# Four of 32 counting rounds moved from the opening of the sample attention to the steps behind its last keys

## What is computed

```
score = where(admissible, sum_h wi * relu(qi . ki) * IDX_SCALE, -inf)
_, sel = top_k(score, 256)
s = where(sel_valid, q . k[sel] * HEAD_DIM ** -0.5, -inf)
o = softmax(s) @ v[sel]
```

## Time and profile before

| | |
|---|---|
| median of 3 runs | 2613.73 us (2608.51 to 2617.16) |
| profiled execution | 2612.9 us |
| its span | 2611.0 us |
| sample attention | about 330 to 519 us of the span |
| PE busy in the whole span | 96% |
| DVE, ACT, POOL busy in the whole span | 61%, 40%, 4% |

### The profile page before, as it was taken

One profiled execution on the slowest core, in us unless ns is written; L12 is line 12 of the kernel. 1 busy time (PEld: TensorE's weight loads), 2 busy tenths in 40 slices (PEclk: granted clock), 3 DMA queues, 4 the chain that ended last, 5 costly groups with the idle time before them and its releaser, 6 DMA issues. The chain is left out here.

```text
span 2611.0 us, 47343 instructions
## 1 busy us (share of the span) xinstructions
PE 2518.6 (96%) x18617; PEld 2407.9 (92%) x18648; DVE 1604.3 (61%) x2965; ACT 1055.0 (40%) x1732; POOL 106.9 (4%) x135
## 2 busy tenths in 40 slices
PE   8899988899999999999999999989999999999998
PEld 7799956577899999999999999989999999999998
DVE  6667876777557666666534466764766666663422
ACT  5567686586534322222312343553422232231201
POOL 1310023200000000000000000000000000000000
PEclk9899999999999999999999999999999999999999
DMA  6312389820123222222513213234142222261312
GB/s 206 86 49 76 113 303 372 331 95 1 34 84 105 74 81 77 85 76 74 207 56 102 86 57 111 72 90 160 59 134 77 74 74 74 74 223 38 113 49 77
DMA packets 256893, 282.59 MB, mean 108 GB/s; under 512 B 18856, under 2 KB 212650, under 8 KB 248557
## 3 DMA queue, kind: packets, MB, share of 16 engines
q1 hardware_dynamic: 244893, 205.09, 24.5%
q0 software_dynamic: 11776, 75.50, 7.9%
q10 hardware_dynamic: 80, 0.02, 0.0%
HBM read 226.51 MB, written 54.06 MB: 107 GB/s over the span
## 5 line engine op out<-in xcount | busy, mean ns | idle before, releaser
L1138 PE MATMUL ffn_acc<-trunk_x_ahead,trunk_w_hi 128*128 128x272 f32 x2464 | 470.6, 290 | 1.0 <-PEq L87 1.0
L1138 PE MATMUL ffn_acc<-ffn_x_later,ffn_w_hi_more 128*128 128x272 f32 x2112 | 398.0, 287 | 5.4 <-DVE ffn_t_u L950 3.4
L1138 PEld LDWEIGHTS ffn_acc<-trunk_x_ahead,trunk_w_hi 128*128 128x128 f32 x2464 | 389.2, 190 | 1.1 <-issue 1.1
L1138 PE MATMUL ffn_acc<-trunk_x_ahead,trunk_w_lo 128*128 128x272 f32 x1232 | 356.0, 289 | 0.0
L1188 PE MATMUL ffn_acc<-trunk_x_ahead,trunk_w_hi 128*128 128x364 f32 (+1 forms) x1344 | 346.4, 327 | 0.7 <-DVE ffn_x_later L1073 0.7
L1138 PEld LDWEIGHTS ffn_acc<-ffn_x_later,ffn_w_hi_more 128*128 128x128 f32 x2112 | 331.9, 189 | 6.3 <-issue 6.2
L1138 PE MATMUL ffn_acc<-ffn_x_later,ffn_w_lo_more 128*128 128x272 f32 x1056 | 304.4, 288 | 0.0
L1188 PE MATMUL ffn_acc<-trunk_x_ahead,trunk_w_lo 128*128 128x364 f32 (+1 forms) x768 | 251.0, 327 | 0.0
L1085 DVE TENSOR_TENSOR trunk_xT<-ffn_acc,trunk_xT 128x364 f32<-128x364 f32 x144 | 76.3, 534 | 274.4 <-PE ffn_acc L1188 274.4
L1188 PEld LDWEIGHTS ffn_acc<-trunk_x_ahead,trunk_w_hi 128*128 128x128 f32 x1344 | 239.2, 188 | 1.3 <-DVE ffn_x_later L1073 1.3
L1138 PEld LDWEIGHTS ffn_acc<-trunk_x_ahead,trunk_w_lo 128*128 128x128 f32 x1232 | 233.9, 190 | 0.0
(11 more groups left out here) (493 smaller groups left out, 5431.6 us busy)
## 6 DMA issues: line engine op xcount, KB each, us to landing
trunk_w_raw<-in_ffn_w_gu SPq DMA_DIRECT2D x88, 512.0 KB, 4.1
a_kept<-trunk_xT SPq DMA_DIRECT2D x88, 272.0 KB, 4.4
trunk_w_raw<-in_ffn_w_down SPq DMA_DIRECT2D x32, 512.0 KB, 3.7
x_saved<-trunk_xT SPq DMA_DIRECT2D x24, 544.0 KB, 2.7
trunk_x_ahead<-a_kept SPq DMA_DIRECT2D x24, 544.0 KB, 6.7
ffn_x_later<-a_kept SPq DMA_DIRECT2D x20, 544.0 KB, 6.9
trunk_w_raw<-in_sg_w_in SPq DMA_DIRECT2D x16, 512.0 KB, 4.0
attxm_w_raw<-in_att_w_in SPq DMA_DIRECT2D x14, 512.0 KB, 5.5
```

The source lines that it names most:

```text
L1138: last = nc.tensor.matmul(bank(2 * PAIR[p] + c)[:, 0:QC], w[:, k * P:(k + 1) * P], x(p, k)[:, c * QC:(c + 1) * QC], start=FRESH[p] and k = ...
```

## The change

`hosts` leaves out the steps 2, 4, 6 and 8 and goes on to step 35: round 2 is now in step 3, round 3 in 5, round 4 in 7, round 5 in 9, and each later round four steps behind its old place. The level is settled in the steps 36 and 37 instead of 32 and 33, and the six pieces of the masks are in the four steps 38 to 41 instead of the six steps 34 to 39. No instruction is added or taken away.

```diff
-    hosts = list(range(BANKS))
+    hosts = [S for S in range(BANKS + 4) if S not in (2, 4, 6, 8)]
     assert len(hosts) == Search.ROUNDS
+    SETTLED = hosts[-1] + 1
     rounds_of = {S: [n for n, x in enumerate(hosts) if x == S] for S in range(LAST)}
-    masks_of = {BANKS + 2 + i: x for i, x in enumerate((((0, 0),), ((0, 1),), ((0, 2),), ((1, 0),), ((1, 1),), ((1, 2),)))}
+    masks_of = {SETTLED + 2 + i: x for i, x in enumerate((((0, 0), (1, 0)), ((0, 1),), ((0, 2), (1, 1)), ((1, 2),)))}
+    assert max(masks_of) < LAST
...
-                if step == BANKS:
+                if step == SETTLED:
                     early.next_level(nc, dve, Search.ROUNDS - 1)
                     early.settle_next(nc, dve)
                     early.settle_count(nc, dve, (0, 1))
-                if step == BANKS + 1:
+                if step == SETTLED + 1:
                     early.settle_count(nc, dve, (2, 3))
                     early.settle_level(nc, dve)
```

## The result

Measured side by side on one chip, the changed kernel took 2617.03 us (median of 22 runs, 2611.16 to 2622.99) and the kernel before 2611.90 us (22 runs, 2607.80 to 2617.55). The medians are 5.1 us apart. The estimate of the ratio, which is not the quotient of the two medians, is 1.0017 with a 95% interval of 1.0011 to 1.0024: 4.4 us more, or 2.9 to 6.3. That is a small loss, within the 0.3% that the prediction called no change, and within its range. The profiled execution took 2618.39 us with a span of 2616.6, against 2612.9 and 2611.0.

A forecast was written before the change was run, and what follows sets the result against it. Opening bound by a latency chain through the odd steps, middle by gathers, tail by DVE's order. Terms -0.9 + 3.9 = +3.0 us on 2613.7 gave 2616.7 us; own range 2615.5 to 2618.5, 8 in 10 within 2610 to 2622.

The forecast's parts named there:

- I cost steps 1 to 8 at a gain of 0: Opening: leaving out the even rounds gives 0, since the 7.07 us loop through the odd steps remains.
- Gain: 0.9 us: Step 8: with no count ahead of the key copies, the exponential's table load and step 9 come 0.9 us earlier.
- the odd loop: Opening: latency chain from step 3's scores through level, count and key copies to step 5's scores, 7.07 us per two steps.
- Does it last?: Middle: an opening 0.9 us shorter starts the full stream of gathers 0.9 us earlier; cost there 0.
- Loss: 3.9 us: Tail: four more rounds on DVE, 7.16 us, less 4.1 us of idle time, plus 0.8 us of new waits.
- the term for ACT: Tail, steps 33 to 35: ACT is slower than DVE by 0.48 us a step; DVE waits some 0.8 us in sum.
- the third piece of the second rival: Start of prompt attention: 6.2 us more at PE's half speed cost 3.1 us, whole +7.8; 7 of the rival's 20% pass that.
- the throughput-bound opening: Rival, opening: ACT's work is the bound, so fewer rounds gain 5.0 us, whole -1.1, 2612.6 us; 17%.
- the tail that hides it all: Rival: moved rounds cost nothing behind step 31 and the opening gives 5.0 us, 2608.7 us; 4%.
- The lower clock through the tail: Second rival: PE stays at the lower clock, tail costs 5.6 us, net +4.7, up to 2621.5 us with the next stage; 20%.

The follow-up runs named there:

- the first kernel with added rounds: Against the changed kernel: all rounds kept in the opening, four idle rounds added in steps 32 to 35; 2613.42 us, 1.0035 of before.
- the second with added rounds: The same kernel, four idle rounds in steps 32 to 35 and all opening rounds kept, measured again: 2610.21 us, 1.0017 of before.

## Why the prediction was right

The forecast was 2616.7 us, and 2617.03 came out, but part of that is chance: the kernel before ran at 2611.90 beside it, 1.8 below its median of the three runs. The difference is the fairer test: +3.0 predicted, +4.4 measured (2.9 to 6.3). Sign and mechanism held; the size is at the lower edge of what was measured. The two terms measured -0.6 and +4.05 where -0.9 and +3.9 were forecast, so the sum of the stage was 0.45 us too low.

- **"I cost steps 1 to 8 at a gain of 0": right.** The odd steps stayed 7.14 us apart, and with all even rounds left out ACT's busy time fell from 44.06 us over the whole opening to some 37.5, for 0.61 us.
- **"Gain: 0.9 us": right in place, too large.** The table load comes 365.29 - 341.56 = 23.73 us behind the scores of step 1, where it was 364.88 - 340.56 = 24.32: 0.59 us earlier, not 0.88. Two turns of the odd loop took 0.07 us more each, and the key copy ahead of the load ends 365.28 - 362.98 = 2.30 us behind the scores of step 7, where I had 364.0 - 361.83 = 2.2.
- **"Does it last?": it did.** The opening kept its 0.6 us to the bank of step 12. Of the middle I can say only that 0.57 us less is far inside its scatter.
- **"Loss: 3.9 us": measured 4.05,** and 31.14 to 31.15 us in four profiles with these four rounds at any clock from 0.94 up. DVE's 7.16 us are 6.94 (28.93 - 21.99), and the idle time of 4.1 us was used up as said. The rest, 4.05 - 6.94 + 4.1 = 1.2 us, is new idle time where the forecast had 0.8 us of waits for ACT. Only 0.43 us of it is such a wait, once and not in each of three steps; the rest is in gaps of at most 0.12 us. So the term for ACT was right in kind and twice too large, the gaps were left out, and the two errors nearly cancel. The third pair's scaling came 9.92 - 8.75 = 1.17 us earlier, where 1.3 was forecast. Against the shorter tail of before's repeat the same four rounds cost 31.15 - 26.58 = 4.57 us.
- **What the sum left out:** the start of the next stage. In the 8 us from the last multiplication on, the granted clock is 0.57 in the changed kernel, and was 0.57 again in its repeat. Before, the same 8 us had this row, with the clock ahead of the DMA share of 0.75:

```profile
518.13:526.13 8.00, 5.91 (x28) 4.83 (x29) 3.21 (x24) 4.28 (x19) 0.00 (x0) 0.79 0.75 212
```

  By 0.57 against 0.79, PE ran at 1.2 GHz for some 6.9 us of it instead of 3.4. In this pair of profiles 0.5 us goes with it: the first block of the prompt attention starts 3.87 us later than before, the ninth 4.37. It is the third piece of the second rival, at a sixth of its price. But it is not the change's alone: from the first block to the ninth it is 9.03 us before and 9.52 in the changed kernel, and 9.66 in the repeats of both. Only three profiles, none with rounds behind the last keys, have about 9.0 there; the other four with none or two have 9.53 to 9.66, and the seven with four 9.52 to 9.98. The clock in the 8 us is 0.50 to 0.59 in those seven, 0.69 to 0.82 in six of the seven with none or two, and 0.61 in the one with two rounds and the last scaling earlier. PE's wait of 3.11 us for the last scaling comes right ahead of this stretch. With the last scaling earlier it was 1.58 us and the clock still 0.59, but PE then waited 1.97 us more for the next stage, so the runs don't tell what decides it.

Added up: -0.6 + 4.05 = +3.45 us is located in the stage, and with the 0.5 us of this pair +3.95. Both lie in the first interval, 2.9 to 6.3; in that of the repeat, 3.7 to 8.3, only the larger. Whether the 0.5 and 2 us by which the two estimates exceed 3.95 are real is open: from the start of the prompt attention to the end the profiles scatter by 7 us, though the kernels are the same there.

The rivals: the throughput-bound opening is refuted by the runs with even rounds and with one round left out; the tail that hides it all, by every run with four rounds behind the last keys. The lower clock through the tail didn't come: 1.00 and 31.15 in the repeat, 0.85 and 31.80 at the worst. Its price of 5.6 us does not come out of the terms given: a scaling 1.3 us earlier, at 500.5, then 7 x 2.91 + 3 us, then the 1.45 us that before had from its last scaling to the next stage, end 6.0 us behind before's stage. And the range of 2610 to 2622 is not widened by 2 us at its top, where 2621.5 + 2 would be 2623.5. Nothing that was measured hangs on either.

## What to carry to other kernels

An engine that is 93% busy may wait in every step and not be the bound: measure one turn of the loop from its own start to its own start, and find the instruction of each engine in it; work that is taken from beside that chain only lengthens a wait that is already there. When work is moved into idle time, add up the idle time of the engine that must take it, and move no more than that: here 4.1 us held two rounds of 1.79 at no cost beyond the scatter of the tail, and each of the next two cost about 2. Before reordering the end of a stage, see what ends it on every engine: the output was ready 0.67 us earlier, but another engine's last write let the next stage begin only 0.3 us earlier. And repeat the profile of the kernel before, too: the slower start of the next stage looked like a cost of the change, and stood in the repeat of before as well.

## What the runs showed of the hardware

**The clock can fall behind a wait of 2.2 us.** In the repeat of before, PE waited 2.23 us for the keys of step 9, and the 4 us behind show a clock of 0.59; the scores take 1.80 us instead of 1.06:

```profile
363.34 1.06 PE L3506 MATMUL satt_tr<-trunk_ident,cache_ring 128*128 128x128 f32 x8 [2.23 <-ACT satt_KT L3618]
364.55 1.80 PE L3520 MATMUL satt_sc<-satt_KT,satt_qs 128*32 128x512 f32 x8
```

```profile
364.00:368.00 4.00, 4.00 (x21) 2.11 (x20) 1.40 (x6) 3.42 (x9) 0.00 (x0) 0.59 0.64 248
```

No other stretch of its opening has a lower clock, and the opening is 47.07 us against 45.48. It also befell the first kernel with added rounds (2.25 us, clock 0.62, opening 47.06), but neither the first profile of before nor the second with added rounds, with the same wait. In the changed kernel that wait is 1.49 us (the row below is from its repeat), and in none of the ten profiles of kernels with fewer rounds there did the clock fall in the opening:

```profile
364.72 1.06 PE L3508 MATMUL satt_tr<-trunk_ident,cache_ring 128*128 128x128 f32 x8 [1.49 <-ACT satt_KT L3620]
```

So with a wait near 2.2 us the clock fell in 2 of 4 profiles, and the opening was 1.6 us longer in both. The Trainium skill ("TensorE: Matmul & The Clock Gate", Part 1) has activity release the throttled clock; the fall behind idle time agrees, and no run here tells what decides between the two cases. If it comes in half of the executions of before, the change would save 0.8 us on average that the profile shown does not have; the times don't show that.

**The pace of the gathers is not a constant.** The middle, where the DMA engines are at 0.97, took between 96.5 and 105.9 us for the same gathers. The median of the kernel before was 2598.95, 2605.11, 2606.12 and 2611.90 us in the four comparisons, and its order is much that of the middle: 13 us between the comparisons is three times what the change does, so kernels are compared with the kernel before on the same chip alone.
